# A hybrid layer on one core: rotary tables earlier, the decayed-query product in a chain of its own, decay rows fetched from DRAM by a broadcast transfer

## The reference

```python
g = jnp.cumsum(g, axis=-1)                       # per head, chunks of tokens
diff = g[..., :, None] - g[..., None, :]
decay = jnp.where(causal, jnp.exp(jnp.where(causal, diff, 0.0)), 0.0)
L = jnp.where(strict, jnp.einsum('bhnid,bhnjd->bhnij', kb, k) * decay, 0.0)
a_intra = jnp.einsum('bhnid,bhnjd->bhnij', q, k) * decay
q_dec = q * jnp.exp(g)[..., None]
k_dec = k * jnp.exp(g_last[..., None] - g)[..., None]
...
ang = positions.astype(jnp.float32)[..., None] * inv_freq   # partial_rope
cos = jnp.cos(ang); sin = jnp.sin(ang)
```

## Time and profile before

| | |
|---|---|
| median of 3 runs | 2395.76 us |
| the profiled execution's own time | 2397.57 us |
| its span, first to last instruction | 2395.8 us |
| PE busy | 2345.4 us (98% of the span) |
| DVE / ACT / POOL busy | 1258.9 / 1072.3 / 1137.0 us |
| mean granted TensorE clock, share of full | 0.989 |

### The profile page before, as it was taken

How to read it: one execution, slowest core, us unless ns; L and a number is a source line. 1 busy time by engine, 2 the same in 40 slices (tenths; PEclk the granted TensorE clock), 3 DMA queues, 4 the chain that set the end, 5 groups by cost and what they waited for, 6 DMA issues and landing times.

```text
span 2395.8 us, 33548 instructions
## 1 busy us (share of the span) xinstructions
PE 2345.4 (98%) x13040; PEld 1893.0 (79%) x13040; DVE 1258.9 (53%) x2473; ACT 1072.3 (45%) x2287; POOL 1137.0 (47%) x836
## 2 busy tenths in 40 slices
PE   8999999999999999999999999999999999999998
PEld 6777777777888888877878787778888888877886
DVE  5877764663451111168767646733566631565153
ACT  6566543544354233246656435443542332444442
POOL 3343323334667556453334333346676664544444
PEclk9999899999999999999999999999999999999999
DMA  4211112122323233221111121223234333364322
GB/s 145 69 57 51 53 45 70 64 71 71 97 80 97 97 97 97 96 84 67 53 54 62 45 71 62 71 80 99 86 97 128 125 123 95 109 185 135 97 97 79
DMA packets 76510, 207.31 MB, mean 87 GB/s; under 512 B 16704, under 2 KB 27712, under 8 KB 75840
## 3 DMA queue, kind: packets, MB, share of 16 engines
q1 hardware_dynamic: 76352, 205.18, 26.6%
HBM read 194.66 MB, written 10.49 MB: 86 GB/s over the span
## 4 chain that ended last, share of the span: by engine, by line
PE 84%; DVE 8%; ACT 4%; issue 1%; POOL 1%; DMA 0%; SPq 0%; DVEq 0%; ACTq 0%
PE ps L991 24%; PE ps L993 23%; PE ps L992 23%; PE ps L2025 1%; PE ps L1953 1%; PE ps L2037 1%; PE ps L1976 1%; PE ps L1972 1%; ACT wH L938 1%; PE ps L2031 1%; ACT prob L1475 1%; DVE x L1002 1%; PE ps L2002 1%; DVE hL L1006 1%; DVE vs L1786 1%
## 5 line engine op out<-in xcount | busy, mean ns | idle before, releaser
L945 POOL TENSOR_TENSOR wL<-raw,wH 128x512 fp32r<-128x512 f32 x660 | 904.1, 1391 | 1047.0 <-ACT wH L938 1046.7
L938 ACT ACTIVATE wH<-raw 128x512 fp32r<-128x512 f32 x660 | 379.6, 623 | 729.3 <-PE ps L993 726.1
L991 PE MATMUL ps<-hH,wH 128*128 128x512 f32 x1584 | 655.4, 414 | 5.3 <-DVE tmp L1783 3.6
L993 PE MATMUL ps<-hH,wL 128*128 128x512 f32 x1584 | 622.0, 393 | 0.0
L992 PE MATMUL ps<-hL,wH 128*128 128x512 f32 x1584 | 621.0, 392 | 0.0
L991 PEld LDWEIGHTS ps<-hH,wH 128*128 128x128 f32 x1584 | 299.5, 189 | 70.4 <-issue 12.6
L993 PEld LDWEIGHTS ps<-hH,wL 128*128 128x128 f32 x1584 | 299.0, 189 | 65.7
L992 PEld LDWEIGHTS ps<-hL,wH 128*128 128x128 f32 x1584 | 300.2, 189 | 50.9 <-issue 0.7
L991 PE MATMUL ps<-OH,wH 128*128 128x512 f32 x576 | 227.3, 395 | 1.0 <-POOL OL L1350 0.7
L993 PE MATMUL ps<-OH,wL 128*128 128x512 f32 x576 | 224.3, 389 | 0.0
L992 PE MATMUL ps<-OL,wH 128*128 128x512 f32 x576 | 224.3, 389 | 0.0
(11 more groups left out here) (433 smaller groups left out, 3433.7 us busy)
## 6 DMA issues: line engine op xcount, KB each, us to landing
raw<-w SPq DMA_DIRECT2D x345, 512.0 KB, 3.3
mats<-matsD SPq DMA_DIRECT2D x4, 1408.0 KB, 6.7
x<-xT SPq DMA_DIRECT2D x8, 256.0 KB, 6.4
matsD<-Cd SPq DMA_DIRECT2D x8, 256.0 KB, 2.5
matsD<-wide SPq DMA_DIRECT2D x4, 512.0 KB, 3.4
mats<-lagsD SPq DMA_DIRECT2D x32, 64.0 KB, 5.9
outT<-acc SPq DMA_DIRECT2D x8, 256.0 KB, 2.2
matsD<-tab SPq DMA_DIRECT2D x8, 128.0 KB, 2.2
```

What stands on the lines that cost most here:

```text
L938: act.activation(weights_at(slot)[0][:, k, :], raw[:, n % RAW, k, :], ACT.Copy).then_inc(high_done, 1)
L945: pool.tensor_tensor(low[:, k, :], raw[:, n % RAW, k, :], high[:, k, :].bitcast(F32), ALU.subtract).then_inc(low_done, 1)
L991: pe.matmul(out, wh, rH[:, t, :], start=(t == 0), stop=False)
L993: mm = pe.matmul(out, wl, rH[:, t, :], start=False, stop=(t == depth - 1))
```

## The change

Four things are changed.

1. Rotary tables: step `cast`, the first of R, needs the end of G instead of the end of D of head 4.
2. `qdec` leaves chain D and becomes a chain Q of its own with its own semaphore, `query_stage`. It needs `exps` of its head (and the scan step that frees its slot). `gramk` follows `exps` directly. What needed D alone and reads or writes the same buffers now needs Q too, and `exps` of a head needs Q of the head before.
3. The stage `rows` of D, with its four transposes a head, is gone. Instead, once a layer, one more matmul in `cumsum` makes the cumulative sums of all heads as 32 rows of 128, DVE copies them out of PSUM (`copyr`, into `gclT`), SP writes them to DRAM by four transfers (8 x 128 each) into `yD`, and for each head SP reads one row of 512 values back into all 128 partitions of `rna` by one transfer. These SP steps are a chain GR.
4. `diff` reads `rna` in SBUF instead of `psD` in PSUM and waits for the transfer, and `exps` turns `rna` into its exponential in place.

```diff
-D_STAGES = [..., "copyv", "rows", "diff", "exps",
-            "qdec", "gramk", "maskk", "first", "gramq", "maskq"]
+D_STAGES = [..., "copyv", "diff", "exps",
+            "gramk", "maskk", "first", "gramq", "maskq"]
+Q_STAGES = ["qdec"]
+ROWS = [(-1, "out"), (-1, "outlanded")] + [(h, s) for h in range(HEADS) for s in ("in", "landed")]
...
         if (kind, j, s) == ("R", 0, "cast"):
-            out = [last("D", 4)]
+            out = [last("G", 0)]
...
+        if kind == "GR" and s == "out":
+            out.append(("G", 0, "copyr"))
+        if kind == "GR" and s == "in" and j:
+            out.append(("Q", j - 1, "qdec"))
...
-            if s == "rows" and j == 0:
-                out.append(last("G", 0))
+            if s == "diff":
+                out.append(("GR", j, "landed"))
...
+        if kind == "Q":
+            out.append(("D", j, "exps"))
+            if TAKEN[j] is not None:
+                out.append(("B", TAKEN[j], "o"))
+        if (kind, s) == ("D", "exps") and j:
+            out.append(("Q", j - 1, "qdec"))
...
+        gclT = osqs[0][0:CH * HEADS, 0:P]
...
+                        elif kind == "GR" and s == "out":
+                            sp.wait_ge(gate_stage, G.before(0, "copyr") + 1)
+                            for c in range(CH):
+                                sp.dma_start(yD[layer, 0:HEADS, c * P:(c + 1) * P], gclT[c * HEADS:(c + 1) * HEADS, :]).then_inc(rows_out, 16)
+                        elif kind == "GR" and s == "in":
+                            if j == 0:
+                                sp.wait_ge(rows_out, 16 * CH)
+                            else:
+                                sp.wait_ge(query_stage, Q.end(j - 1))
+                            sp.dma_start(rna[:, :], yD[layer, j:j + 1, :].to_broadcast([P, SEQ])).then_inc(rows_in, 16)
...
-                        elif kind == "D" and s == "qdec":
-                            pool.wait_ge(gram_stage, D.before(j, s))
+                        elif kind == "Q":
+                            pool.wait_ge(gram_stage, D.before(j, "exps") + 1)
...
-                                act.activation(rna[:, :], psD[:, 0, :], ACT.Exp)
+                                if j:
+                                    act.wait_ge(query_stage, Q.end(j - 1))
+                                act.activation(rna[:, :], rna[:, :], ACT.Exp)
...
+                            elif s == "copyr":
+                                ins = v.tensor_copy(gclT, psD[0:CH * HEADS, 0, P:2 * P])
...
+                                v.wait_ge(rows_in, 16 * (h + 1))
...
-                                    ins = v.scalar_tensor_tensor(out=DT[:, c, :], in0=a0[:, c, :], scalar=gcl[:, i:i + 1],
+                                    ins = v.scalar_tensor_tensor(out=DT[:, c, :], in0=chunks(rna[:, :])[:, c, :], scalar=gcl[:, i:i + 1],
                                                                  in1=k_("later"), op0=ALU.subtract, op1=ALU.min)
...
+                                ins = pe.matmul(psD[0:CH * HEADS, 0, P:2 * P], gg, k_("upper"), start=True, stop=True)
...
-                                elif s == "rows":
-
-                                    ins = pe.transpose(psD[:, 0, cc], gcl[:, i:i + 1].to_broadcast([P, P]), ident)
```

58 lines of the change are left out of this document (33 added, 25 removed), and 2 rows, old and new, of the table special.

## The result

The changed kernel is slower, not faster: ratio of its time to the kernel before 1.0022, 95% interval 1.0016 to 1.0028. The median of 20 runs is 2402.08 us against 2396.49 us. That is 5.6 us up where 16 us down were forecast, and outside the range. The profiled execution of it took 2399.15 us, 3 us less than its median, and that of the kernel before 2397.57 us. Of the ten runs of the changed kernel above 2402.1 us all but one have a mean granted clock of 0.987 or 0.988, where the profiled one has 0.989; that fits the rest, but no trace of them was kept.

What follows compares the result with a forecast made beforehand. PE was taken as the bound, busy 2345 of 2396 us. Gains of 6.7 + 1.8 + 18.6 less 10.8 for new waits gave 16.3 us off, forecast 2380 us, with an 8 in 10 range of 2367 to 2392.

Steps and rivals of the forecast that it cites:

- the tables' stalls: Layer 0, near 260 and 308 us: PE waits of 5.0 and 4.05 us plus low clock, all taken as gone.
- The transposes: 64 row transposes leave PE, 7.0 us counted in full, less 0.3 us for added steps: 6.7 us gain.
- `qdec` beside the chain: `gramk` no longer waits for POOL, so PE's waits in four places go: 1.8 us gain.
- The tables: Layer 0, 219.9 to 321.4 us: moving DVE's 16 table instructions away ends both stalls and their low clock, 18.6 us gain.
- where they land: Table work moved to 52 to 58 us and heads 1 to 3 of layer 0 is covered; booked at nothing.
- New tight places: Adjacent inverse steps in layer 0 head 1 and layer 1 head 2: waits plus one clock fall, 10.8 us loss.
- Rows from DRAM: Row transfers out to DRAM and back land before `diff` needs them in each head; hidden, booked at nothing.
- rival E: Rows arrive late and DVE, then PE, stand at `diff`; 16 heads at 2 us, 2412 us; 4%.
- `diff` from SBUF: `diff` with two SBUF inputs may be slower, at most 26 us of DVE; nothing booked on PE's path.
- rival D: POOL locks out `diff` on DVE, all 26 us reaching PE's path: 2406 us; 4%.
- Rival B: Tables make two like stalls in heads 0 to 3, or new places cost their upper bound: 2385 to 2387 us; 25%.
- rival C: Tables and rows do nothing; new waits of 3 to 8 us take back the transposes' gain: 2391 to 2395 us; 9%.

Runs made afterwards that it cites:

- e12: Kernel before with only the planner's booked cost for the row transposes changed (0.75 for 0.45), both layers planned anew, same instructions; ratio 0.9938 to the kernel before.
- e1: Changed kernel's data path, tables late, in the kernel before's order of steps in both layers; ratio 0.9981 to the kernel before.
- e6: Changed kernel with layer 0 in its new order and layer 1 in the order of the kernel before; ratio 0.9966 to the kernel before.
- e6b: Changed kernel with layer 0 in the order of the kernel before (late tables) and layer 1 in the new order; ratio 1.0034 to the kernel before.

## Why the prediction was wrong

Two steps of the forecast failed. In layer 0 it took the tables' stalls off for good and booked their landing place at nothing, and in the sum it put the waits that a new plan brings at 10.8 us. In the traces layer 0 came out at 5.7 us of gain, where its terms give 14.6 to 19.7, and layer 1's part at 9.3 us of loss, where they give 1.7 of gain to 3.4 of loss.

**The transposes** (6.7 us net): their size on PE was about right, 6.2 us less of busy time. That "they count in full" was not shown: with the decayed queries they brought 4.6 us in the old order, where 8.5 were booked. New waits took 2.4 us, 1.7 of them behind `DT`, and more low clock in that trace up to 1.7.

**`qdec` beside the chain** (1.8 us): the wait for POOL went as said; 2.4 us of waiting for ACT's `DT` came at the like places.

**The tables** (18.6 us) and **where they land** (nothing): the step that failed in layer 0. That both stalls would go was right, and the clock there is 1.00. But stalls came where the tables went. Between 50 and 160 us PE is idle for 8.1 us, 2.2 before, and the clock was low for 17.0 us in two stretches that end by 162 us, where before it was not low at all; the forecast had named a fall of the clock in 60 to 160 us as a sign that it is wrong. Over layer 0 PE's idle time fell by 1.9 us only and the low clock by 6.9 us. The cause as I had it, DVE's table work by itself, is not right either: e12 has the tables in the late stretch and neither stall. What the twelve plans show is that early tables bring stalls to the early heads in every plan, and that the plan decides how large they are.

**New tight places** (10.8 us) failed in size and in number, and this is the step that failed in layer 1. Head 1 of layer 0: 2.7 us booked for two steps, 2.70 measured, by luck as said; but the third wait, 2.1 us, and a low-clock stretch of 10.2 us with a second one of 6.8 us near 77 us weren't in it. Head 2 of layer 1: 3.0 booked, 6.9 measured, and the clock fell there too, the second fall that I had kept as an upper bound. Not foreseen at all: 1.98 us for `DT` near 1099, 2.26 us for `S` near 1147, 1.71 us for `Y` near 1271. Over layer 1's part PE is idle for 19.9 us, 10.7 before, which is the whole loss of 9.3; its busy time is 600.5 for 600.4, since the clock is low for 17.0 us, 6.8 before, and that took back what the transposes gave. That it is the order and not the data path is shown by e1, e6 and e6b (608.9 and 609.3 in the old order, 620.6 in the new one); whether the new chains or chance made this order worse stays open. I had looked for rows of steps without weight matmuls on PE's list; the costly waits came from the queues of ACT and DVE, which that list does not show.

**Rows from DRAM** (nothing) and **rival E**: right, 3.2 us to land and no wait. **`diff` from SBUF** and **rival D**: `DT` took 36 ns more in the changed kernel and 142 ns more in e1, each under the 0.33 us from which it would decide. Booked at nothing on PE's path, it has waits of 1.7 us together right behind it in e1, and in the changed kernel it has a part in one wait of 1.98 us. The Trainium skill, "SBUF — State Buffer", section "Who interferes with whom", lets such a cost be expected. The traces agree: of 16 groups of four `DT` instructions only those beside POOL's `wL` are longer, by 0.6 to 1.9 us a group in e1, and only with the input in SBUF; over the run that is 2.3 to 9.3 us of DVE.

**Rival B** said that the tables, now in heads 0 to 3, make stalls there like the two before. For layer 0 that is what came, and by its terms layer 0 gains 3.8 us, where 5.7 came. But both it and rival C booked too little for new waits: none let layer 1 lose by its order. The forecast gave 8% to slower, all of it to mechanisms of the new data path, and none to the plan itself, though the change to the kernel's code also moved some 200 of 1440 PE steps in each layer.

## What to carry to other kernels

Where a program writes the order, an edit is two changes: the work, and a new draw of the order. Before forecasting the first, measure how much the second scatters (change one booked cost, keep the instructions), and time the edit in the old order too; here the new data path was worth 4.6 us, and the same instructions in four plans lay 26 us apart.

A stall that overlaps some extra work in time is not shown to come from it, and one plan that has the work and no stall does not clear it either: here only twelve plans side by side showed that stalls come to the early heads with the tables, and that in the mean the move gains nothing. To find what a single wait is made of, follow the wait back through every in-order queue to the step that was late, and ask what stood ahead of it. Filling the waiting engine with other work only moves the wait if the late step is elsewhere.

## What the runs showed that I had not expected

The last part, from the mark near 1650 us on, has the same instructions in the same order in every kernel, and it takes 741.5 to 742.2 us in ten traces, 747.1 to 747.6 in eight, and 743.4 and 743.7 in two. The difference between the first two is one low-clock stretch of 13.7 us some 490 us into it. Two windows over the same work, e6 and then e1:

```profile
2130.00:2160.00 30.00, 27.52 (x187) 22.14 (x185) 23.86 (x37) 12.27 (x19) 11.50 (x8) 1.00 0.59 177
```
```profile
2136.00:2166.00 30.00, 28.65 (x151) 22.78 (x150) 20.32 (x34) 11.58 (x18) 10.01 (x8) 0.77 0.51 153
```

The wait ahead of it is 1.35 us in both. The single times of e6 lie in two heaps, which fits, seven from 2385.3 to 2388.4 and five from 2393.2 to 2397.0 us, those of before less clearly. So a change of 5 us can't be read from one execution, and the same waits bring the clock down in one run and not in the next.
